# Turning the sample probabilities in blocks of four and five instead of singly between the value products

## The reference

```
# branch A: 8 query heads, 2 key heads, only the top-k selected keys count
s = einsum('bqgrd,bqkgd->bqgrk', q, kv[:, :, :, 0]);  p = softmax(where(valid, s, -inf))
o_a = einsum('bqgrk,bqkgd->bqgrd', p, kv[:, :, :, 1])
# branch B: 4 heads, two softmaxes each, over all cached and new keys
a = p[:, :, 0] - lam * p[:, :, 1]
o_b = rmsnorm(einsum('bhqs,bshe->bqhe', a, v)) * (1 - lam_init)
# then, for all 1056 tokens
h = h + rmsnorm((sigmoid(g_a) * (o_a @ w_br_a) + sigmoid(g_b) * (o_b @ w_br_b)) @ w_out)
h = h + rmsnorm((silu(gate) * up) @ w_down);  h = h + sigmoid(h @ w_ple_gate) * (p_i @ w_ple_proj)
```

## Time and profile before

| | |
|---|---|
| three runs | 2984.07, 2984.15, 2989.68 us; median 2984.15 us |
| the profiled execution | 2989.68 us, span of its trace 2988.1 us |
| busy in the span | PE 2807.8 us (94%), weight loads 1990.2 (67%), DVE 1400.4 (47%), POOL 676.3 (23%), ACT 586.2 (20%) |
| mean granted TensorE clock | 0.978 |
| DMA | 706 MB, 236 GB/s over the span |

### The profile page before, as it was taken

The page is one execution under the profiler, slowest core; times in us unless marked ns, Lnnn a source line. Parts: engine busy times, 40 slices in busy tenths (PEclk is TensorE's granted clock), DMA queues, the critical chain, the costliest instruction groups (busy, mean ns, idle before and its releaser), DMA issues.

```text
span 2988.1 us, 69660 instructions
## 1 busy us (share of the span) xinstructions
PE 2807.8 (94%) x27060; PEld 1990.2 (67%) x27060; DVE 1400.4 (47%) x2685; ACT 586.2 (20%) x1285; POOL 676.3 (23%) x1190
## 2 busy tenths in 40 slices
PE   7998979999888889999998989999899899999998
PEld 5774534666566666677766667777667676777898
DVE  2436868988577635433244353433434532102211
ACT  2441112100466401101011111010111201001101
POOL 0131002200300000143343333433334334440000
PEclk9999989999999999999999999999999999999999
DMA  6567229621700486899999989999899897763686
GB/s 212 167 186 229 85 70 333 217 72 65 222 8 12 116 268 206 271 331 320 327 340 328 320 288 333 333 321 328 299 339 342 295 330 256 239 233 116 224 266 201
DMA packets 411396, 706.03 MB, mean 236 GB/s; under 512 B 69217, under 2 KB 226017, under 8 KB 410946
## 3 DMA queue, kind: packets, MB, share of 16 engines
q1 hardware_dynamic: 325298, 467.93, 47.8%
q0 software_dynamic: 75456, 232.86, 23.3%
q10 hardware_dynamic: 10320, 0.84, 0.3%
HBM read 659.40 MB, written 90.00 MB: 251 GB/s over the span
## 4 chain that ended last, share of the span: by engine, by line
PE 56%; DVE 2%; DMA 2%; SPq 1%; ACT 1%; issue 1%; DVEq 1%; ACTq 0%; POOLq 0%; POOL 0%
PE sa_t L1685 43%; PE sa_s L2044 5%; PE sa_o L2109 4%; PE sa_s L2054 1%; DMA tw_w<-packed 1%; PE sa_stat L2084 1%; PE sa_o L2113 1%; DVE tw_rstd L1760 1%; DVE sa_key_b L2226 1%; PE sa_t L1655 0%; SPq L1999 0%; ACT sa_raw L2173 0%; DVE tw_h L1769 0%; DVEq L1768 0%; DMA y<-tw_y_row 0%
## 5 line engine op out<-in xcount | busy, mean ns | idle before, releaser
L1986 POOL DMA_DIRECT2D sa_ring_v<-cache_b_kv x512 | 275.2, 537 | 1048.0 <-PE sa_o L2113 702.3
L2226 DVE STREAM_TRANSPOSE sa_key_b<-sa_ring_k 128x2048 f32<-128x2048 f32 x128 | 294.9, 2306 | 242.0 <-PE sa_s L2044 212.5
L1685 PE MATMUL sa_t<-tw_z,early_w 128*128 128x304 f32 (+1 forms) x1664 | 392.1, 391 | 5.9 <-DVE tw_z L1771 3.9
L1685 PE MATMUL sa_t<-tw_z,tw_w 128*128 128x304 f32 (+1 forms) x1664 | 389.9, 389 | 1.5 <-DVE tw_sig L1774 1.3
L1685 PEld LDWEIGHTS sa_t<-tw_z,early_w 128*128 128x128 f32 x1664 | 285.8, 191 | 95.9 <-issue 18.4
L1685 PEld LDWEIGHTS sa_t<-tw_z,tw_w 128*128 128x128 f32 x1664 | 283.9, 190 | 88.7 <-issue 12.9
L1987 POOL DMA_DIRECT2D sa_ring_va<-cache_a_kv x512 | 274.1, 535 | 54.0 <-issue 27.4
L485 PE MATMUL pr_acc<-pr_w,pr_u_t 128*128 128x512 f32 (+1 forms) x640 | 256.0, 545 | 0.0
L1012 PE MATMUL sel_g<-sel_u,sel_gw 128*128 128x352 f32 x768 | 227.5, 459 | 0.0
L1012 PEld LDWEIGHTS sel_g<-sel_u,sel_gw 128*128 128x128 f32 x768 | 146.0, 190 | 81.7 <-issue 0.8
L2044 PE MATMUL sa_s<-sa_key_b,sa_q_pad 32*32 32x256 f32 x8192 | 182.5, 397 | 7.8 <-issue 4.1
(11 more groups left out here) (347 smaller groups left out, 3839.6 us busy)
## 6 DMA issues: line engine op xcount, KB each, us to landing
sa_ring_k<-cache_b_kv SPq DMA_DIRECT2D x512, 256.0 KB, 5.4
sa_ring_v<-cache_b_kv POOLq DMA_DIRECT2D x512, 256.0 KB, 6.2
early_w<-packed SPq DMA_DIRECT2D x168, 512.0 KB, 5.7
tw_w<-packed SPq DMA_DIRECT2D x168, 512.0 KB, 5.9
sa_ring_ka<-cache_a_kv SPq DMA_DIRECT2D x512, 64.0 KB, 5.5
sa_ring_va<-cache_a_kv POOLq DMA_DIRECT2D x512, 64.0 KB, 6.0
packed<-w_gate_up POOLq DMA_DIRECT2D x44, 512.0 KB, 15.4
gate_t<-sel_gate SPq DMA_DIRECT2D x16, 528.0 KB, 3.0
```

The costliest lines, as they stand in the source:

```text
L1685: ins = pe.matmul(out, self.w[at % self.SLOTS][:, first + k - lo, :], src[:, cols], start=(k == 0), stop=(k == depth - 1))
L1986: pool.dma_start(ring_v[:, n % RING, :], rows_of(cache_b, page, 1)).then_inc(v_in[n // 4 % 2], 16)
L2226: nc.vector.transpose(key_b[:, at:at + 4].rearrange("p g n s -> p (g n s)"), ring_k[:, at:at + 4, :].rearrange("p g e -> p (g e)")).then_i ...
```

## The change

The turns of a half are no longer spread over two steps. Before, half 0 of a batch had turns 0 and 1 in the step with `s % 8 == 1`, around the part 1 of its values, and turns 2 and 3 in the next step, around part 0, with the sums behind; half 1 did the same in the steps with 5 and 6, with turn 4 last. Now the four turns of half 0 and the sums stand together at the end of the step with `s % 8 == 1`, behind `finish`, and the five turns of half 1 at the end of the step with 5. The waits follow: a half's first values product waits for the half's last turn (on PE), and a half's first copy waits for the last values product of the half before (on ACT). The number of turns, copies, products and loads is unchanged.

```
+            if s % PER == 1 and s > PER:
+                step += [("finish", b - 1)] if b else []
+                step += [("turn", b, 0, i) for i in range(4)] + [("sum", b)] if b < NB else []
+            if s % PER == 2 and s > 2 * PER:
+                step += [("combine", b - 1)]
+            if s % PER == 5 and s > PER:
+                step += [("turn", b, 1, i) for i in range(5)]
...
-            turns = s > PER and b < NB and s % PER in (1, 2, 5, 6)
-            half, ending = s % PER // 4, s % 4 == 2
-            step += [("turn", b, half, 2)] if turns and ending else []
             step += [("values", s - LAG, 0)] if s >= LAG else []
-            step += [("turn", b, half, 3)] if turns and ending else []
             step += [("keys", s, 1)] if s < CHUNKS else []
             step += [("top_rows", b)] if ends else []
-            step += [("turn", b, half, 0)] if turns and not ending else []
             step += [("values", s - LAG, 1)] if s >= LAG else []
-            step += [("turn", b, half, 1)] if turns and not ending else []
             step += [("keys_a", s)] if s < CHUNKS else []
             step += [("spread", b)] if ends else []
-            step += [("turn", b, 1, 4)] if turns and ending and half else []
-            step += [("finish", b - 1)] if s % PER == 1 and s > 2 * PER else []
-            step += [("sum", b)] if turns and ending and not half else []
-            step += [("combine", b - 1)] if s % PER == 2 and s > 2 * PER else []
...  values(), tensor engine
-                if j == 0:
-                    pe.wait_ge(stat_read, use["turn", b, half, 2 * part + 1] + 1)
-                if v % PER == PER - 1 and part == 1:
-                    pe.wait_ge(stat_read, use["turn", b, 1, 4] + 1)
+                if j == 0 and part == 0:
+                    pe.wait_ge(stat_read, use["turn", b, half, 3 + half] + 1)
...  prob_out(), scalar engine
-                if n in (0, 2) and (b or half):
-                    act.wait_ge(v_used, (b * PER + 4 * half) * CH - (4 if n == 0 else 0))
-                if n == 4 and b:
+                if half == 0 and b and n == 0:
                     act.wait_ge(pv_done, b)
+                if half == 1 and n == 0:
+                    act.wait_ge(v_used, (b * PER + 4) * CH)
```

## The result

The changed kernel takes 3038.35 us (median of 4 runs, 3036.61 to 3046.61), the kernel before 2984.11 us in the runs beside it. The ratio is 1.0178, with a 95% interval of 1.0162 to 1.0194: 54 us slower (48 to 58), where 40 were forecast. The profiled execution took 3034.05 us with a span of 3032.5, 44.4 us above that of before: it was one of the quicker ones and the profiled one of before one of the slower. Outside the sample phase nothing changed. The medians are used for times, the profiles for where they lie.

The account below looks back on a forecast made before the run. PE was taken to bound the sample phase; 30.4 + 5.7 + 3.3 + 1 - 1.3 + 1.3 = +40.4 us on the median 2984.15 gave 3024 us, +1.35%, with an 8-in-10 range of 3005 to 3052.

Parts of the forecast that it names:

- the joints: Where turns adjoin, PE waits for ACT's copy: 40 more such places at 0.76 us, +30.4 us.
- The dearer place of a turn beside dense products, +5.7: Turns moved from beside values or scores products to beside dense products or turns cost PE more: +5.7 us, bounds 0 and 7.2.
- Pages, +3.3: Value parts brought together wait for pages not landed, worst in the last batch: +3.3 us, bounds 0 and +15.
- Cover of the norm, +1: Before the norm's waits PE has two turns less to do meanwhile: +1 us, bounds 0 and 3.
- the old wait of 6.4: PE's 6.4 us wait for a copy goes as a line; the norm's next dense product takes it over: 0.
- The fold, -1.3: In four places a step now stands between the sums and the fold of `combine`, ending 1.3 us of wait: -1.3.
- The clock, one fall: PE's clock falls once, in the one run of four turns: +1.3 us, bounds 0 and 14.3.
- the rival with 13 to 36 us from the blocks: Clock falls of 1.3 us at 11 to 29 places in the blocks of turns, about 3050 us; chance 0.20.
- absorbed: New waits only move PE's 58 us of idle in the sample phase, time stays 2984 to 2990 us; chance 0.04.
- faster because the transfers bound: Page transfers set the pace, joints cost nothing and POOL loads earlier: 2974 us; chance 0.04.

Follow-up runs that it names:

- doubled copies: Every turn's copy from PSUM done twice: in the changed kernel 3072.0 us (88 above before), in the kernel before 2982.03 us (ratio 1.0003).
- kernel without joints and pages: Changed kernel with one dense unit between every two turns of a block and branch A's value loads left out from the ninth page on: 2982.41 us.
- pair without the loads: Branch A's value loads left out from the ninth page on, in both kernels: the kernel before 2976.79 us, the changed kernel 3004.78 us.
- spaced kernel: Changed kernel with one dense unit put between every two turns of a block and before the sum: 3024.13 us, ratio 1.0142.

## Why the prediction was right in the main, and where it was short

*PE bounds the phase, and the joints lie open:* right. The price of 0.76 us a joint came from one place in the trace; in the block, turns are 1.33 us apart where one takes 0.58, that is 0.75. The forecast of 28 us of waits in about 40 places met 29.3 in 42. The doubled copies show that they are on the path.

*The dearer place of a turn beside dense products, +5.7:* neither shown nor refuted. The kernel without joints and pages stands 4 us above its counterpart, within the error.

*Pages, +3.3:* here the sum was short, and it is the term that makes 40 into 54. The 4.4 us priced at the worst place were 4.95. What failed is "three to five other chunks have about as much time as the issue and landing of four pages need; at the median landing they wait for nothing". The wait came at twelve places, ten of them new, in every batch of values but the second, and pages are worth 26 us. Two mistakes are in the step. The only landing time that it shows is the last batch's, 4.3 us at the median, while between 1190 and 2500 the median was 6.2 us or more. And a median is too short a measure, since a part waits for the last landing of its eight loads: at the seven new waits before 2500 that one came 6.5 to 8.2 us behind the last issue, where the parts are due 5.8 to 6.9 us behind it. And it counted POOL's four issues from the part that frees them, while POOL can still have the other part's four ahead, eight in a row from 1409.9 to 1421. The term's upper bound, +15, was short too: it held no price for the clock behind a wait.

*Cover of the norm, +1, and the old wait of 6.4 taken over in full:* the sign was wrong. That wait is gone and the waits of the norm's products did not grow by it; PE's waits for DVE and ACT in the dense rest fell from 23 to 15 us: with three copies ahead of the norm's work, ACT reaches that work earlier. That reason is argued from the order, not shown, and its worth was not measured by itself.

*The fold, -1.3:* right, its line is gone from the waits.

*The clock, one fall:* three falls are visible at blocks, at 1437, 1819 and 2204, each worth about 1.5 us; the term was a few microseconds short. The mean over the whole run is 0.978 in both kernels, but a mean over the run cannot tell, since the time at the lower level outside the phase differs as well (83 us before, 63 now). In the phase alone the time at the lower level grew from 51 to 68 us, which is worth some 8 us, and without the loads it did not grow. So the rival with 13 to 36 us from the blocks does not stand. Falls behind long page waits, seen at 2568, belong to the pages.

*The sum:* that 40 came within 14 us of 54 is in part luck, since two errors offset each other. Without the pages the sum forecast 37 us, and the pair without the loads shows 28; the pages were forecast at 3 and are worth 26.

*The rivals* "absorbed" and "faster because the transfers bound": refuted together by the doubled copies, which cost 34 us with joints and nothing without. But the thought behind the second, that transfers are near the bound, was nearer to the truth than its chance of 0.04: the pages did not bound, but they were next in line.

None of the versions that compute the right result beats the kernel before. The most that page waits could give back to it is about what leaving out a fifth of the values' bytes gave, 5 us, at the edge of what can be measured.

## What to carry to other kernels

Work that hides another engine's answer must be looked at in pairs: two steps that use one PSUM tile cost nothing while something stands between them, and the whole copy when they adjoin. The same work often covers a second thing in the other direction; before moving it, take for each load the time from its landing to its use, in the same stretch of the trace, and compare that surplus with what the move takes from between. Here most places had some 3 to 4.5 us to spare, and the move took 4 to 5. And a gap closed with work from the next step opens there: the spaced kernel gave back half of its gain in weight and page waits.

## What was not expected of the hardware

Dropping seven eighths of the bytes of one small load (64 KB of 320 KB a page), with its issue still made, took 15 us off, and dropping the issue as well 16 more, though POOL is busy only 35% of the phase (550 of 1575 us). POOL's share says little here, because its issues come eight in a row, 1.51 us a page, and the last one decides. PE's load of weights for a waiting turn again began only with the wait's end, in the same instant as the matmul at all 42 waits; the 1.33 us between turns contain it.
